# Branch B with its values stationary: two head pairs a step, probabilities scaled before their transposes

## The reference

```python
s = jnp.einsum('bnqgrd,bnkgd->bngrqk', qb, kb).astype(jnp.float32) * scale + bias
s = jnp.where(mask[None, :, None, None], s, NEG_INF)
m = jnp.maximum(jnp.max(s, axis=-1, keepdims=True), sink)
e = jnp.exp(s - m)
p = e / (jnp.sum(e, axis=-1, keepdims=True) + jnp.exp(sink - m))
o = jnp.einsum('bngrqk,bnkgd->bnqgrd', p, vb.astype(jnp.float32))
...
merged = jax.nn.sigmoid(ga) * (ya @ w_branch_a[l]) + jax.nn.sigmoid(gb) * (yb @ w_branch_b[l])
```

## Time and profile before

| | |
|---|---|
| median of 3 runs | 1996.26 us (1995.23 to 1996.38) |
| span of the profiled execution | 1992.9 us |
| the median less that span | 3.4 us |
| PE busy | 1900.4 us, 95% |
| DVE, ACT, POOL busy | 953.2, 611.9, 468.3 us |
| branch B, scores of the first to scores of the last step | 562.20 to 800.60 us |
| first product of gate tile gb1 | 822.76 us |

### The profile page before, as it was taken

The page is one execution under the profiler, slowest core; times in us unless marked ns, Lnnn a source line. Parts: engine busy times, 40 slices in busy tenths (PEclk is TensorE's granted clock), DMA queues, the critical chain, the costliest instruction groups (busy, mean ns, idle before and its releaser), DMA issues.

```text
span 1992.9 us, 25360 instructions
## 1 busy us (share of the span) xinstructions
PE 1900.4 (95%) x9498; PEld 1561.9 (78%) x9498; DVE 953.2 (48%) x2203; ACT 611.9 (31%) x1352; POOL 468.3 (23%) x243
## 2 busy tenths in 40 slices
PE   3999999999989999999999999999999999999996
PEld 2777777777778888788888878888888888888884
DVE  7267666667655556210241346533334343333437
ACT  4345555455544444321122231211111111111104
POOL 5111011111011111122221220243333223333314
PEclk9999999999999999899999999999999999999998
DMA  4511111111110110013422251121121111112102
GB/s 161 188 51 45 31 44 34 33 44 41 32 30 15 30 30 22 22 43 105 139 85 74 85 192 51 32 85 43 42 69 47 52 42 42 42 42 68 48 0 85
DMA packets 143113, 117.95 MB, mean 59 GB/s; under 512 B 23284, under 2 KB 129964, under 8 KB 143020
## 3 DMA queue, kind: packets, MB, share of 16 engines
q1 hardware_dynamic: 133804, 112.51, 17.9%
q10 hardware_dynamic: 9216, 4.20, 0.7%
HBM read 99.87 MB, written 21.53 MB: 61 GB/s over the span
## 4 chain that ended last, share of the span: by engine, by line
PE 85%; DVE 7%; ACT 3%; issue 1%; DMA 1%; SPq 1%; POOL 1%; POOLq 0%; DVEq 0%; ACTq 0%
PE bank L449 24%; PE bank L450 23%; PE bank L451 23%; PE bank L486 4%; PE bank L473 4%; PE bank L571 3%; PE bank L518 2%; ACT mix L795 1%; DVE mix L1101 1%; PE bank L572 1%; DVE res L1032 1%; DMA w_raw<-in_w_in_dram 1%; PE bank L519 1%; DVE small L1160 1%; DVE o_buf L1075 1%
## 5 line engine op out<-in xcount | busy, mean ns | idle before, releaser
L449 PE MATMUL bank<-hT_hi,w_hi 128*128 128x512 f32 x1312 | 528.1, 402 | 4.8 <-DVE hT_lo L998 3.0
L450 PE MATMUL bank<-hT_lo,w_hi 128*128 128x512 f32 x1312 | 515.3, 393 | 0.0
L451 PE MATMUL bank<-hT_hi,w_lo 128*128 128x512 f32 x1312 | 514.6, 392 | 0.0
L912 POOL TENSOR_TENSOR w_lo<-w_raw,w_hi 128x1024 fp32r<-128x1024 f32 x67 | 161.0, 2403 | 712.0 <-ACT w_hi L696 712.0
L449 PEld LDWEIGHTS bank<-hT_hi,w_hi 128*128 128x128 f32 x1312 | 250.0, 191 | 61.4 <-issue 5.3
L451 PEld LDWEIGHTS bank<-hT_hi,w_lo 128*128 128x128 f32 x1312 | 248.8, 190 | 53.9
L450 PEld LDWEIGHTS bank<-hT_lo,w_hi 128*128 128x128 f32 x1312 | 249.7, 190 | 48.4
L1279 DVE TENSOR_TENSOR res<-res,bank 128x512 f32<-128x512 f32 x224 | 154.0, 687 | 141.2 <-PE bank L451 141.2
L449 PE MATMUL bank<-y_hi 128*128 128x512 f32 x512 | 199.5, 390 | 2.7 <-DVE small L1296 2.7
L450 PE MATMUL bank<-y_lo,y_hi 128*128 128x512 f32 x512 | 199.2, 389 | 0.0
L451 PE MATMUL bank<-y_hi,y_lo 128*128 128x512 f32 x512 | 199.2, 389 | 0.0
(11 more groups left out here) (128 smaller groups left out, 2939.7 us busy)
## 6 DMA issues: line engine op xcount, KB each, us to landing
w_raw<-in_w_in_dram SPq DMA_DIRECT2D x100, 256.0 KB, 3.3
w_raw<-in_w_ff_dram SPq DMA_DIRECT2D x64, 256.0 KB, 3.0
mix<-in_w_ff_dram SPq DMA_DIRECT2D x16, 1024.0 KB, 7.2
bias_rows<-bias_line SPq DMA_DIRECT2D x3, 1536.0 KB
res<-in_x_dram SPq DMA_DIRECT2D x8, 512.0 KB, 7.8
h_spill<-res SPq DMA_DIRECT2D x8, 512.0 KB, 6.8
o_spill<-o_buf ACTq DMA_DIRECT2D x64, 64.0 KB, 1.6
w_raw<-in_w_branch_b_dram SPq DMA_DIRECT2D x16, 256.0 KB, 3.9
```

What stands on the lines that cost most here:

```text
L449: pe.matmul(bank, lhs[0], rhs[0], start=start, stop=False)
L450: pe.matmul(bank, lhs[0], rhs[1], start=False, stop=False)
L451: return pe.matmul(bank, lhs[1], rhs[0], start=False, stop=stop)
L912: pool.tensor_tensor(w[1][:, n % 2], w_raw[:, :, :], w[0][:, n % 2].bitcast(F32), ALU.subtract).then_inc(w_lo_done, 1)
```

## The change

- A step takes two head pairs (four heads) and one query tile, instead of one pair and two tiles. There are 4 × 8 = 32 steps as before, and the same number of scores and projection groups. For this the order of the query tiles' groups becomes half 0 of two tiles, then half 1 of both (`ORDER`, `POS`), in all engines.
- The sink is a 193rd column of the scores (`set_sink`, a small POOL copy two steps ahead), so that one Exp with its sum covers it. The maximum and the sink are joined and negated in one DVE instruction. Six small DVE and ACT instructions a step (L1160, L1161, L1163, L833, L1168, L1170) become two.
- POOL multiplies the probabilities by the reciprocal of their sum before the transposes (two instructions, 256 and 512 elements a partition), into a buffer of their own.
- The 64 keys of the previous tile of two heads share one transpose: 6 transposes in place of 8 (4 in tile 0).
- The values are stationary: for the tile's own keys once with the second half of the columns zero, once with the first, and for the previous tile's 64 keys both heads stacked in the rows (`v_main`, `v_side`, with zeros that POOL writes first). The transposed probabilities of two pairs move, 256 columns. Nine products (six in tile 0) in place of 16. Their result is channel by token, so the `yb` transposes go: ACT copies the bank to `res` (`o_rows_b`), and after the loop ACT and DVE split `res` into high and low part, 1024 columns a tile.
- The value products are those of two steps before, behind the transposes of the step before. The projection's half group comes directly behind the scores. DVE's `qk_lo` moves ahead of the reciprocal.
- POOL's and ACT's weight splits stand in steps 2 and 4 of every eight, one tile each. In branch A's last head the last group is now half 0 of qb1 instead of half 1 of qb0.
- The bias of two pairs is loaded together, into `bias_b_buf` and, for every second, `o_buf`.

The diff, cut to its core:

```diff
+B_STEPS = B_PAIRS // 2 * NT
+ORDER = []
+for _n, (_kind, _i) in enumerate(TILES):
+    if _kind != "qb":
+        ORDER += [(_n, 0), (_n, 1)]
+    elif _i % 2 == 0:
+        ORDER += [(_n, 0), (_n + 1, 0), (_n, 1), (_n + 1, 1)]
+POS = {o: g for g, o in enumerate(ORDER)}
+B_GROUP = POS[(TILE[("qb", 0)], 1)]
...
-BATCHES += [("pb", j, s, b) for j in range(B_PAIRS) for s in range(NT // 2) for b in range(2)]
-BATCHES += [(kind, t, b) for kind in ("yb", "ya", "h1") for t in range(NT) for b in range(2)]
+BATCHES += [("pb", s, b) for s in range(B_STEPS) for b in range(2 if s % NT else 1)]
+BATCHES += [(kind, t, b) for kind in ("ya", "h1") for t in range(NT) for b in range(2)]
...
@@ views
+        bias_b = [t[:, 0:768].rearrange("p (j m k) -> p j m k", j=2, m=2) for t in (bias_b_buf, o_buf)]
+        v_main = [t[:, 4:6, :].rearrange("p s k -> p (s k)")[:, 0:NT * 192].rearrange("p (t c) -> p t c", t=NT) for t in y]
+        v_side = [t[:, 7, :].rearrange("p (t c) -> p t c", t=NT) for t in y]
+        pT_b = [[t[:, slot, 0:768] for t in y] for slot in (3, 6)]
+        q_b = [t[:, 0:2, :].rearrange("p h (j q) -> p h j q", j=2) for t in y]
+        s_b = mix[:, 0:2, :].rearrange("p s k -> p (s k)")[:, 0:1568].rearrange("p (s c k) -> p s c k", s=2, c=4)
+        p_b = mix[:, 2:4, 0:768]
...
@@ batch_views, "vb"
+                return ([(v_main[part].rearrange("p t (g e) -> p t g e", e=HD)[:, tiles, 0:3:2, :], bank.rearrange("p t (g e) -> p t g e", g=2))]
+                        + [(v_side[part][g * HD:(g + 1) * HD, tiles, g * HD:(g + 1) * HD], bank[CHUNK:P, :, g * HD:(g + 1) * HD]) for g in range(2)])
...
@@ tensor
+            def scores_b(s):
+                g, i = s // NT, s % NT
+                half, at = i // 4, i % 4 * P
+                if i % 4 == 0:
+                    pe.wait_ge(freed_dve, freed(False, POS[(TILE[("qb", 2 * g + 1)], half)]))
+                scores([SCORE[("b", g, i, m, 0)] for m in range(2)], 0,
+                       [([t[:, half, j, at:at + P] for t in q_b], slice(i * P - CHUNK if i else 0, (i + 1) * P), j * 192 + (0 if i else CHUNK))
+                        for j in range(2)])
+            def transposes_b(s):
+                pe.wait_ge(pb_scaled, s + 1)
+                for b in range(2 if s % NT else 1):
+                    transposes(("pb", s, b))
+            def attend_b(s):
...
+                values = [[t[:, i, 0:P] for t in v_main], [t[:, i, CHUNK:192] for t in v_main]]
+                if i:
+                    values.append([t[:, i - 1, :] for t in v_side])
+                for n, v in enumerate(values):
+                    mm = three(PV[:, 0:2 * P], v, [t[:, n * 2 * P:(n + 1) * 2 * P] for t in pT_b[s % 2]], n == 0, n == len(values) - 1)
+            for s in range(B_STEPS):
+                scores_b(s)
+                group(*ORDER[B_GROUP + s // 2], range(s % 2 * 4, s % 2 * 4 + 4))
+                if s >= 1:
+                    transposes_b(s - 1)
+                if s >= 2:
+                    attend_b(s - 2)
+            transposes_b(B_STEPS - 1)
+            attend_b(B_STEPS - 2)
+            attend_b(B_STEPS - 1)
...
@@ scalar
+            for s in range(B_STEPS):
+                slot, first = s % 2, 0 if s % NT else CHUNK
+                act.wait_ge(max_ready, A_HEADS * NT + s + 1)
+                act.wait_ge(sink_set, s + 1)
+                for c in range(4):
+                    e = act.activation(s_b[:, slot, c, first:193], s_b[:, slot, c, first:193], ACT.Exp,
+                                       bias=neg_max4[:, slot, c:c + 1], accum_out=sums4[:, slot, c:c + 1])
+                e.then_inc(exp_done, 1)
+                if s % 2 and TILES[ORDER[B_GROUP + s // 2][0]][0] == "qb":
+                    group_hi(*ORDER[B_GROUP + s // 2])
+                if s >= 1:
+                    probs_hi(s - 1)
+                if s >= 2:
+                    o_rows_b(s - 2)
+                if s % NT in (2, 4):
+                    split_weights(TILE[("qb", 0)] + s // NT * 2 + s % NT // 2 + 1)
...
+                        act.wait_ge(ob_read, B_STEPS)
+                        act.activation(y[0][:, c, :], res[:, c, :], ACT.Copy).then_inc(yb_hi, 1)
...
@@ gpsimd
+            for s in range(B_STEPS):
...
+                if s % NT:
+                    pool.tensor_tensor(p_b[:, slot, HALF:768].rearrange("p (c k) -> p c k", c=4), s_b[:, slot, :, 0:CHUNK],
+                                       inv4[:, slot, :].unsqueeze(2).broadcast_to([P, 4, CHUNK]), ALU.mult)
+                pool.tensor_tensor(p_b[:, slot, 0:HALF].rearrange("p (c k) -> p c k", c=4), s_b[:, slot, :, CHUNK:192],
+                                   inv4[:, slot, :].unsqueeze(2).broadcast_to([P, 4, P]), ALU.mult).then_inc(pb_scaled, 1)
+                if s + 2 < B_STEPS:
+                    set_sink(s + 2)
+                if s % NT in (2, 4):
+                    split_weights(TILE[("qb", 0)] + s // NT * 2 + s % NT // 2 + 1)
...
@@ vector
+            for s in range(B_STEPS):
...
+                dve.scalar_tensor_tensor(neg_max4[:, slot, :], mx4[:, slot, :], -1.0, neg_sink[:, g, :], ALU.mult, ALU.min).then_inc(max_ready, 1)
+                if s % 2 and TILES[ORDER[B_GROUP + s // 2][0]][0] == "qb":
+                    qk_lo(*ORDER[B_GROUP + s // 2])
+                dve.wait_ge(exp_done, A_HEADS * NT + s + 1)
+                dve.reciprocal(inv4[:, slot, :], sums4[:, slot, :]).then_inc(inv_ready, 1)
+                if s >= 1:
+                    probs_lo(s - 1)
...
+                dve.wait_ge(yb_hi, c + 1)
+                dve.tensor_tensor(y[1][:, c, :], res[:, c, :], y[0][:, c, :].bitcast(F32), ALU.subtract).then_inc(yb_lo, 1)
```

More of the change, by code:

```diff
@@ L293, in batch_views @@
             if kind == "pb":
[L294 to L297, removed]
+                _, s, b = batch
+                width = 512 if b == 0 else 256
+                return [(pT_b[s % 2][part][:, 512 * b:512 * b + width], TR[n % 2][:, 0:width])]
             if kind == "va":
@@ L453, in group @@
             def group(n, half, kts=range(KT)):
-                g = 2 * n + half
+                g = POS[(n, half)]
                 if kts[0] == 0:
@@ L474, in transposes, with scores @@
                 mm.then_inc(tr_done, 1)
-            def scores(kind, h, i, c, pieces):
-                units = [SCORE[(kind, h, i, m, c)] for m in range(2)]
+            def scores(units, k_slot, pieces):
                 if units[1] >= 3:
@@ L485, in scores @@
                             rows = slice(m * HD, (m + 1) * HD)
-                            mm = pe.matmul(SC[units[m] % 3][:, at:at + keys.stop - keys.start], q[left][rows, h % 2, queries],
-                                           k[right][rows, h % 2 if kind == "a" else 0, keys], start=not (left or right), stop=left == 1)
+                            mm = pe.matmul(SC[units[m] % 3][:, at:at + keys.stop - keys.start], queries[left][rows],
+                                           k[right][rows, k_slot, keys], start=not (left or right), stop=left == 1)
                             if left == 1 and at == pieces[-1][2]:
@@ L590, in _ @@
-            pe.wait_ge(exp_done, A_HEADS * NT + B_PAIRS * NT // 2)
-            for b in range(2):
-                transposes(("pb", B_PAIRS - 1, NT // 2 - 1, b))
-            attend_b(B_PAIRS - 1, NT // 2 - 1)
+            def scores_b(s):
[6 more added lines that the diff above has]
+                        for j in range(2)])
@@ L601, in _ @@
                         pe.wait_ge(y_rows, c + 1)
-                    for b in range(2):
-                        transposes(("y" + kind, c, b))
+                        for b in range(2):
+                            transposes(("ya", c, b))
                     for half in range(2):
@@ L838, in _, with o_rows_b, probs_hi @@
-            for b in range(2):
-                batch_hi(("pb", B_PAIRS - 1, NT // 2 - 1, b))
+            act.wait_ge(spilled, 16 * NT)
+            def o_rows_b(s):
+                g, i = s // NT, s % NT
+                act.wait_ge(pv_done, A_HEADS * NT + s + 1)
+                act.activation(res[:, 2 * g:2 * g + 2, i * P:(i + 1) * P], PV[:, 0:2 * P].rearrange("p (j q) -> p j q", j=2), ACT.Copy).then_inc(ob_read, 1)
+            def probs_hi(s):
+                for b in range(2 if s % NT else 1):
+                    batch_hi(("pb", s, b))
@@ L841, in out_hi @@
+            probs_hi(B_STEPS - 1)
+            for s in (B_STEPS - 2, B_STEPS - 1):
+                o_rows_b(s)
             def out_hi(n):
@@ L932, in _ @@
             split_weights(1)
-            for n in range(2, TILE[("gb", 1)] + 1):
+            for n in range(2, TILE[("qb", 1)] + 1):
                 split_weights(n)
@@ new lines, in _, with set_sink @@
+            for part in range(2):
+                pool.memset(v_side[part].bitcast(F32), 0.0).then_inc(v_zero, 1)
+            pool.wait_ge(pv_done, A_HEADS * NT)
+            for part in range(2):
+                pool.memset(v_main[part][:, :, HD:P].bitcast(F32), 0.0).then_inc(v_zero, 1)
```

(3 more changed lines are left out.)

271 lines of the change are left out of this document (106 added, 165 removed).

## The result

The changed kernel takes 1934.4 us (median of four runs, 1928.5 to 1935.9), the kernel before 1995.7 beside it (1994.8 to 1996.4): a ratio of 0.969, 95% interval 0.968 to 0.970. The forecast was 1937, its range 1923 to 1956.

The account below looks back on a forecast made before the run. The prediction took branch B's loop to be bound by TensorE's issue. Savings of 56.3 us up to gb1 and 4.7 behind it, less 1.6 for a clock drop, made 59.4 off 1996.26: 1937 us, range 1923 to 1956.

Parts of the forecast that it names:

- A step: Branch B's loop: scores 0.85, projection 2.93, transposes 0.64, value products 1.21, together 5.63 us against 7.33 before.
- Waits in the loop from step 2 on: TensorE's waits ahead of scores and transposes in branch B's loop, 14.1 us in all.
- The lock: POOL's 2.40 us weight splits hold the small negated maximum on DVE until they end; the loop pays about 12 us.
- The clock: One clock drop of 1.6 us stays after the waits of the start, as the kernel before had there.
- The start: End of branch A and first steps of B: new waits delay TensorE, step 2 starts at 574.9.
- the wait for w_lo: Ahead of branch A's last projection group: TensorE waits 2.06 us for the low part of qb1's weights.
- The end: From the last step's scores to gate tile gb1's first product: 15.9 us against 22.16.
- Behind gb1: Six sets of eight yb transposes between gate groups go, 0.79 us each, 4.7 us saved.
- products at 0.17: Rival: value products of branch B start 0.17 us apart, 6 us more, 1943 us; chance 0.12.
- no block: Rival: POOL's splits do not hold the new negated maximum, 12 us less, 1925 us; chance 0.17.
- latency: Rival: the chain from scores to scaled probabilities sets the step at 8.2 us, 2003 us; chance 0.03.
- The clock rival: The clock still falls in the loop, one drop each second step, 23 us more, 1960 us; chance 0.17.

Follow-up runs that it names:

- experiment 2: Changed kernel with the previous tile's value product reading only rows 0 to 63, its products between the first block's: 1955.0 us.
- experiment 4: Changed kernel with two more POOL multiplications a step (256 and 240 elements, 1.20 us) ahead of the real ones: 1926.7 us.
- experiment 11: Changed kernel with POOL's weight splits in steps 3 and 5 of eight, behind the negated maximum and ahead of the scaling: 1919.9 us.
- experiments 5: Changed kernel with ACT's and POOL's weight splits in branch B's loop in steps 1 and 3 of eight instead of 2 and 4: 1929.4 us.
- 8: Changed kernel with the edits of experiments 5, 6 and 7 together: 1921.9 us.
- 6: Changed kernel with the split of qb1's weights one step earlier in branch A's last head: 1928.7 us.
- 7: Changed kernel with ACT's Sqrt behind the second gate tile's sigmoids and DVE's reciprocal behind the last low part of yb: 1928.7 us.
- 3: Changed kernel with the sink left out of branch B, so the negated maximum has one tensor operand: 1930.6 us.

## Why the prediction was right

The mechanism held: fewer, full-row products shorten every step, and POOL's splits hold the negated maximum. The sum held too, 60.0 us saved in the profile against 59.4, but that it came so close is luck: some 10 us of terms taken too long (steps 3.2, waits 6.2, the end 0.6) met 9 us taken too short (the clock in the loop 6.3, the start 2.8).

- *A step* of 5.63 measured 5.52: transposes 0.57 (0.64 forecast) and projection 2.87 (2.93), value products 1.24 (1.21). The 0.123 taken for each product was 0.119; the edges cost 0.17, not 0.10. Over 29 steps that is 3 us less. The rule of the Trainium skill that I weighed ("TensorE: Matmul & The Clock Gate", Part 3, "The mechanism": loads overlap only where the row group differs) does not describe these products: nine on the same full rows start 0.12 apart, each with a load of its own, and in experiment 2 it is the change of row height that costs.
- *Waits in the loop from step 2 on,* 14.1 us forecast, measured 7.9. The lock was there as in the earlier trace rows and ended with POOL's split, but the blocked maximum lasted 1.64 rather than 1.9, the wait at step 4 was 1.72 instead of 3.1, those at steps 8, 16 and 24 0.6 instead of 1.16, and no transpose waited (POOL's scaling took 0.61 + 1.04, not 1.9). 6.2 us too much.
- *The clock,* one drop forecast, none of it in the loop. Four came there, one behind each wait of 1.46 to 1.72 us: 6.3 us too little. This is the term that the prediction lacked; as a rival it had one drop in each second step, 23 us. It had also read too much low clock into the kernel before: not about half of its steps are like that of the earlier trace rows but eight of 31 (8.9 to 9.0 us from scores to scores, where 7.3 is the rule), and a ninth, step 1, with waits in it. Steps from 2 to 31: 175.7 − 3.2 − 6.2 + 6.3 = 172.6, measured 172.8.
- *The start:* the wait for w_lo 1.95 (2.06 forecast); the first scores at 565.49 and step 2 at 579.32, where 574.9 stood. The 4.4 us are mostly low clock in branch A's last projection (7.19 instead of 5.57) and in step 1's scores and projection (6.77 instead of 3.72); I had priced one drop of 1.6 for all of it, which leaves 2.8.
- *The end:* 15.3 against 15.9: the last transposes start 5.5 behind the last scores (5.75 forecast), with a wait of 0.7 for the scaled probabilities; gb1's bank is waited for 5.1.
- *Behind gb1:* 4.6 against 4.7.

The rivals: products at 0.17 are refuted by the rows, no block by the 1791 ns, latency by experiment 4. (The first was priced too low: 0.42 more a step over 29 steps is 12 us, of which the seven waits ahead of scores could take up 3, so 9 and not 6.) The clock rival was right in kind at four drops and not fourteen.

That a lock on a 0.16 us instruction was worth about 13 us is shown by experiment 11: 7.0 us of the waits ahead of scores go, and the four drops behind them, 6.3 us.

What decides whether the clock falls behind such a wait stays open. In the seven profiles above with long waits at steps 4, 12, 20 and 28, a wait of 1.46 or more was followed by a low stretch in 4 of 4 cases (the change, twice), 2 of 3 (experiments 5 and 8), 2 of 4 (6 and 7) and 1 of 4 (3), 17 of 26 in all, and the waits of 1.92 and 1.99 at step 4 in experiments 6 and 3 were not. There the waits of 0.64 and less never were. Nor is the length of a wait enough in the kernel before: of its six waits of 0.8 us ahead of value products three (steps 17, 21 and 25) were followed at once by a step 1.6 longer, at 0.81 granted, and behind the other three (5, 9 and 13) the next step ran at full clock and the one after it was the slow one. What the runs of the changed kernel spread by (1928.5 to 1935.9) is about four drops of 1.6; the mean granted clock was 0.989 in the fastest and 0.986 or 0.987 in the others, which fits, but no profile of the fastest run shows the drops missing.

## What to carry to other kernels

Where small products bind TensorE, count them: fewer, with full rows and twice the columns, cost little more each (0.119 us against 0.112), and a change of row height at every product cost more than the empty half of the rows is worth. Before a wide POOL operation is placed, look in the trace which tiny DVE instruction in a chain beside it is held by it, and start the wide one behind it. Between a product and its operand's evacuation leave another step's work: here that distance was worth the whole gain.

## What the runs showed of the hardware

- A change of row height at every product (128 and 64 rows, 256 columns) cost about 0.19 us: 0.31 a product against 0.12 at one height. In the kernel before, with narrower products, the starts lay 0.17 to 0.18 apart at a change and 0.17 without.
- Full-row products of 128 and of 256 columns start 0.112 and 0.119 apart.
- POOL's multiplication with a broadcast operand took 1.04 us for 512 elements, where a subtraction with two full inputs and an fp32r result took 1.30.
- A tensor_scalar of four elements with one SBUF tensor was held for up to 1784 ns by POOL's TENSOR_TENSOR, a scalar_tensor_tensor of the same size up to 2240, a reciprocal inside a split not at all (0.18 us).
- 1.20 us more work a step on POOL made the kernel faster (1926.7 us against 1934.4).
- The low clock behind short waits: it set in behind some waits of 1.5 us and not behind others of the same length, in otherwise busy stretches.
